# Four page products beside each other in the array, head pairs in alternation, and an input projection that starts before the norm

## The chip, the cores and the metric

The kernel runs on one core of one Trainium2 chip. The metric is the device time of one execution in microseconds, the median of several runs. TensorE (PE) multiplies, VectorE (DVE), ScalarE (ACT) and GpSimd (POOL) work element by element, SyncE (SP) issues most transfers.

## The reference

One inference step of a one-layer hybrid decoder, all in float32, for a prompt of 256 tokens and 8 samples of one new token each, whose 256 past keys and values lie in a paged cache (two pages of 128 rows per sample, 16 heads of 64):

```python
proj = rmsnorm(x, g_mix) @ w_in              # 1024 -> q, k, v, z, x/B/C, dt (IN_COLS)
q, k = rope(q), rope(k)
attn = softmax(q @ k.T / 8, causal) @ v      # prompt: own rows; sample: 2 pages of cache + its own new row
xbc  = silu(causal_conv(xbc)); dt = softplus(dt_raw + dt_bias)
y    = ssd_scan(xs, dt, -exp(a_log), B, C, state) + d_skip * xs
y    = group_rms(y * silu(z)) * g_ssd
x    = x + concat(rmsnorm(attn, g_attn), y) @ w_out
# PEER: 8 heads, two product keys of 128, top 16 of 16384 experts per token
x    = x + sum_e softmax_e * gelu(xn . u_e) * v_e
y_out = rmsnorm(x, g_final)                  # also out: new k, v, conv and ssd states
```

For the prompt all 16384 experts are computed densely and weighted; for the samples the chosen rows are gathered.

## The kernel before

Tokens lie along the free axis (264 columns: 256 of the prompt, 8 samples), features along the 128 partitions in 8 chunks. The order of each engine is written out by hand; semaphores tie the engines together.

- **Opening.** ScalarE squares the input `res`, TensorE sums the squares over partitions with a matrix of ones (L466, 8 products), VectorE makes `rstd`, scales the input into `xn` (L903), TensorE forms dt (L471). Then `tile(i)` (L481): 8 products of a 128x128 weight tile from `ring` (four slots, loaded by SyncE) with `xn` into bank `pj[i % 2]`; ScalarE copies it to `proj` (`copy`). Twelve tiles are the convolution's channels (VectorE's `conv`), with small turns and products after tiles 4 and 6. SyncE writes the decay rows and the B/C rows to memory and reads them back spread over all partitions (`wide`), between its tile loads.
- **Chunk loop.** For each of 8 chunks `c` (two heads): four tiles (q, k, v, z), between them `expand`, `turn_probs`, `ends`, `attend` of the chunk before, and at the end `mixed` (the scan's three products for each head) and `scores` (L494 to L496). Each head's results use half of the array's rows or columns.
- **Page stage.** After the loop 32 cache pages of 512 KB pass through six slots (`pages`, `NS = 6`): SyncE's `page(n)` waits until page `n - 6` is used, loads the physical page number from `ptab`, and issues the transfer. `key_pages` (L602) gives the scores of one sample's 16 heads against its two pages (16 rows of output, 256 columns); VectorE and ScalarE make its softmax (`sample_max`, `sample_probs`); `value_pages` (L635) multiplies by the values, with the probabilities padded into 128 columns of which one sample's 16 are not zero, so that all samples add up in two banks. Among them stand the sums of the two norms (L654, L657). VectorE's chain from these sums to the split operands (`mix_low`, L1188) precedes the output projection.
- **Output projection.** `out_half` (L671), 16 weight tiles, each split in a high and a low part by ScalarE and GpSimd. `values` (L681) after its first half tile picks each sample's heads out of `v6`.
- **PEER.** Query tiles and keys, then `up` (L1521) and `down` (L1551) over all experts. Before group `GX` of `down` stands `samples` (L1571, L1582): the samples' residual and their gathered rows, 8 rows of output.

## Time and profile before

| | us |
|---|---|
| median of 3 runs (lowest, highest) | 1233.85 (1231.4, 1236.24) |
| the profiled execution's own time | 1229.45 |
| its span | 1227.3 |
| TensorE busy | 1199.8 |
| VectorE, ScalarE, GpSimd busy | 785.8, 571.5, 753.8 |

The profiled execution lies 4.4 us below the median of the runs. Busy time of TensorE says that it had an instruction in flight, not that its array was full. In the profile every float32 product stands as two instructions, so that `x16` are eight products. PEclk 1.00 is 2.4 GHz, 0.50 is 1.2 GHz.

### The profile page before, as it was taken

The page shows a single profiled execution, that of the slowest core. Times are in us where ns is not written, and L with a number is a line of the kernel's source. Part 1 is how long each engine was busy: PE and PEld are TensorE (multiplying, and loading weights), DVE is VectorE, ACT ScalarE, POOL GpSimd, SP SyncE. Part 2 cuts the span into 40 slices and gives each one's busy share as a digit, 9 for nine tenths or more (in the row PEclk, how much of TensorE's full clock was granted, in tenths as well). Part 3 has the DMA queues.
Part 4 walks back from the last instruction along what each step waited for, and adds up shares of the span by engine and source line. Part 5 has one row for each costly group of instructions (what it writes and reads, how often), then busy time and mean ns, then how long its engine had stood idle before and what let it go on. Part 6 is the DMA issues. An engine that isn't in the chain of part 4 may idle for free.

```text
span 1227.3 us, 23601 instructions
## 1 busy us (share of the span) xinstructions
PE 1199.8 (98%) x7463; PEld 1039.8 (85%) x7463; DVE 785.8 (64%) x1749; ACT 571.5 (47%) x1287; POOL 753.8 (61%) x622
## 2 busy tenths in 40 slices
PE   7999999999999999999999999999999999999997
PEld 5877888745988899999999999998888888888766
DVE  4579787666139999400599999994544555666334
ACT  3222323252435555556555554444555555555435
POOL 0058241003835599998776767666776798798645
PEclk9999999999999999999999999999999999999999
DMA  6565575287645276666544444444665697788523
GB/s 210 164 214 148 166 257 155 88 288 272 184 150 156 88 224 190 188 186 182 162 141 144 142 142 140 145 140 145 189 189 188 188 325 259 238 282 269 184 97 111
DMA packets 99863, 224.88 MB, mean 183 GB/s; under 512 B 11682, under 2 KB 12306, under 8 KB 99274
## 3 DMA queue, kind: packets, MB, share of 16 engines
q1 hardware_dynamic: 96762, 214.52, 56.2%
q0 software_dynamic: 2304, 8.39, 2.0%
q10 hardware_dynamic: 720, 1.01, 0.2%
q8 instruction: 40, 0.66, 0.2%
q14 instruction: 37, 0.30, 0.1%
HBM read 215.61 MB, written 8.19 MB: 182 GB/s over the span
## 4 chain that ended last, share of the span: by engine, by line
PE 68%; issue 1%; POOL 1%; DVE 0%; ACT 0%; DVEq 0%; POOLq 0%; ACTq 0%
PE bank L1551 29%; PE bank L1521 28%; PE bank L1531 5%; PE bank L1474 2%; PE bank L1486 1%; PE bank L1582 1%; PE bank L1498 1%; POOL hl L1399 1%; PE bank L1571 0%; POOL hl L1414 0%; DVE acts L1941 0%; ACT acts L1751 0%; PE bank L1600 0%; PE bank L1564 0%; DVEq L1319 0%
## 5 line engine op out<-in xcount | busy, mean ns | idle before, releaser
L1399 POOL TENSOR_TENSOR hl<-ring,hl 128x512 fp32r<-128x512 f32 x448 | 586.1, 1319 | 195.1 <-ACT hl L1631 186.2
L1631 ACT CAST hl<-ring 128x512 fp32r<-128x512 f32 x512 | 316.8, 620 | 301.0 <-PE bank L1551 168.0
L1521 PE MATMUL bank<-split,hl 128*128 128x256 f32 x3072 | 378.7, 282 | 0.5 <-ACT hl L1631 0.3
L1521 PEld LDWEIGHTS bank<-split,hl 128*128 128x128 f32 x3072 | 366.3, 188 | 1.2 <-POOL hl L1399 0.6
L1551 PE MATMUL bank<-hl,split 128*128 128x512 f32 x1524 | 353.6, 394 | 0.0
L1551 PEld LDWEIGHTS bank<-hl,split 128*128 128x128 f32 x1524 | 285.9, 188 | 67.8 <-issue 0.9
L481 PE MATMUL pj<-xn,ring 128*128 128x264 f32 x704 | 165.0, 390 | 1.4 <-DMA ring<-in_w_ring 1.4
L1911 DVE TENSOR_TENSOR split<-acts,split 128x256 fp32r<-128x256 f32 x128 | 128.1, 1022 | 50.3 <-ACT split L1727 46.5
L481 PEld LDWEIGHTS pj<-xn,ring 128*128 128x128 f32 x704 | 132.3, 192 | 25.7 <-issue 2.8
L1918 DVE TENSOR_TENSOR hl<-ring,hl 128x512 fp32r<-128x512 f32 x64 | 45.1, 705 | 119.8 <-ACT hl L1631 119.8
L457 POOL TENSOR_TENSOR wo<-ring,wo 128x512 fp32r<-128x512 f32 x32 | 46.9, 1473 | 95.5 <-ACT wo L856 95.4
L433 POOL TENSOR_TENSOR hs<-hs,dds 128x256 f32<-128x256 f32 x32 | 22.7, 739 | 116.9 <-DVE xdt L1091 75.5
L1877 DVE TENSOR_SCALAR bv<-bkey,ig 128x130 f32<-128x130 f32 x256 | 86.0, 394 | 0.0
L1886 DVE TENSOR_TENSOR acts<-acts,bank 128x244 f32<-128x244 f32 (+31 forms) x64 | 66.3, 1036 | 19.5 <-PE bank L1531 19.2
L1698 ACT ACTIVATE acts<-bank 128x256 f32<-128x256 f32 (+31 forms) x124 | 41.1, 332 | 67.3 <-PE bank L1521 67.2
L1531 PE MATMUL bank<-bv,av 128*128 128x128 f32 x512 | 67.4, 274 | 0.0
L1531 PEld LDWEIGHTS bank<-bv,av 128*128 128x128 f32 x512 | 62.4, 191 | 0.0
L1414 POOL TENSOR_TENSOR hl<-ring,hl 128x512 fp32r<-128x512 f32 x24 | 31.0, 1301 | 35.9 <-ACT hl L1641 35.7
L1727 ACT CAST split<-acts 128x256 fp32r<-128x256 f32 x128 | 51.0, 401 | 0.2 <-DVE acts L1894 0.2
L728 ACT COPY proj<-pj 128x264 f32<-128x264 f32 x44 | 16.6, 376 | 68.7 <-PE pj L481 68.7
L1894 DVE TENSOR_TENSOR acts<-acts,gtmp 128x256 f32<-128x256 f32 (+32 forms) x67 | 42.0, 626 | 8.4 <-ACT gtmp L1700 8.4
L1873 DVE TENSOR_TENSOR av<-bank,ig 128x512 f32<-128x512 f32 x64 | 43.3, 677 | 0.0
(339 smaller groups left out, 1218.4 us busy)
## 6 DMA issues: line engine op xcount, KB each, us to landing
ring<-in_uv SPq DMA_DIRECT2D x256, 256.0 KB, 2.7
ring<-in_v_rows SPq DMA_DIRECT2D x256, 256.0 KB, 3.1
ring<-in_w_ring SPq DMA_DIRECT2D x76, 512.0 KB, 3.7
room<-in_cache_k SPq DMA_DIRECT2D x16, 512.0 KB, 5.3
room<-in_cache_v SPq DMA_DIRECT2D x16, 512.0 KB, 4.7
hs<-in_state_ssm SPq DMA_DIRECT2D x8, 512.0 KB, 4.7
out_ssm_s<-hs SPq DMA_DIRECT2D x8, 512.0 KB, 5.8
acts<-x_rows SPq DMA_DIRECT2D x8, 512.0 KB, 5.5
```

The source lines that it names most:

```text
L457: nc.gpsimd.tensor_tensor(wo[:, n % HL, 1], raw_o[:, n % RAW], wo[:, n % HL, 0].bitcast(F32), ALU.subtract).then_inc(o_lo, 1)
L481: mm = nc.tensor.matmul(pj[i % 2][:, 0:NT], ring[:, s, k], xn[:, k], start=(k == 0), stop=(k == KD - 1))
L1399: nc.gpsimd.tensor_tensor(hl[:, r % HL, 1], raw[:, r], hl[:, r % HL, 0].bitcast(F32), ALU.subtract).then_inc(lo_done, 1)
L1521: mm = nc.tensor.matmul(out, hl[:, r % HL, m, k * P:(k + 1) * P], split[:, x, kk, 0:TP], start=(kk == 0 and n == 0), stop=(kk == KD - 1 an ...
L1531: mm = nc.tensor.matmul(rb[m % 2][:, j * P:(j + 1) * P], av[:, m % 2, j], bv[:, m % 2, j, 0:P], start=True, stop=True)
L1551: mm = nc.tensor.matmul(acc[2 * k + half][:], split[:, p, 2 * s + a, k * P:(k + 1) * P], hl[:, r % HL, m], start=False, stop=False)
L1631: nc.scalar.copy(hl[:, r % HL, 0], raw[:, r]).then_inc(hi_done, 1)
L1727: nc.scalar.copy(split[:, g % 2, 2 * n, 0:TP], acts[:, g * GRP + n, :]).then_inc(wg_hi, 1)
L1877: hot = nc.vector.tensor_scalar(bv[:, m % 2, j], bkey[:, :, 0:BW // BR], ig[:, 0, at:at + 1], ig[:, 2, at:at + 1], ALU.is_equal, ALU.mult)
L1886: nc.vector.tensor_tensor(a, a, rb[m % 2][:].rearrange("p (t c) -> p t c", t=TG)[:, :, 0:R0 + m + 1], ALU.mult).then_inc(g_out, 1)
L1911: nc.vector.tensor_tensor(split[:, p, 2 * s + 1, 0:TP], acts[:, g * GRP + s, :], split[:, p, 2 * s, 0:TP].bitcast(F32), ALU.subtract).then ...
L1918: nc.vector.tensor_tensor(hl[:, r % HL, 1], raw[:, r], hl[:, r % HL, 0].bitcast(F32), ALU.subtract).then_inc(lo_dve, 1)
```

## The change

Six things are changed.

1. The first two tiles (and dt) use `xg`, the input times `g_mix` alone; VectorE multiplies their results by `rstd` (`evict_early`), in place of ScalarE's copy. The squares are added on VectorE, so that one product sums them. Eighteen 128x128 products of `pick` with itself stand first on TensorE.
2. The small products after tile 4 stand after tile 6, those after tile 6 after tile 7. ScalarE, not SyncE, issues the three row transfers.
3. In `scores`, `attend` and `mixed` the two heads alternate from product to product; `attend` and `mixed` now write 64 rows of output for each head in place of 128.
4. Pages are worked in fours: a batch is page `g` of four samples, and the four products go to output partitions 0, 32, 64 and 96, 16 rows each. The batch's pages are released together (`mm.then_inc(page_used, SIDE)`). A sample's own new key joins the softmax at the end, by two factors per sample and head (`sample_rates`, `sample_factors`) which `spread_rates` spreads over the partitions.
5. The values of the first four samples are picked by `values(0)` before the output projection, the others and the factors after its first half tile.
6. In `samples` the eight samples go to four output positions, two rows each; the banks are cleared first.

```diff
+SIDE, SPAN = 4, 32
+NQ = NB // SIDE
...
-                    b, g = n // NPG % NB, n % NPG
+                    q, g, j = n // (NPG * SIDE) % NQ, n // SIDE % NPG, n % SIDE
+                    b = q * SIDE + j
...
-                    if i == 10:
-                        sp.wait_ge(bc_copied, 1)
-                        sp.dma_start(t["bc_rows"].rearrange("a b n -> b a n"), brow).then_inc(bc_kept, 16)
...
-                        sp.wait_ge(bc_kept, 16)
-                    if i == 9:
-                        sp.wait_ge(acs_ready, 1)
-                        sp.dma_start(t["acs_rows"], acs[:]).then_inc(acs_kept, 16)
...
+                for j in range(SIDE):
+                    sp.dma_start(sel6[j * SPAN:j * SPAN + NH], t["sel"]).then_inc(sel6_in, 16)
...
+                        if i == 0:
+                            pe.wait_ge(xg_done, k + 1)
+                        if i == 2 and k % 4 == 0:
+                            pe.wait_ge(normed, k // 4 + 1)
+                        mm = nc.tensor.matmul(pj[i % 2][:, 0:NT], ring[:, s, k], (xg if i < 2 else xn)[:, k], start=(k == 0), stop=(k == KD - 1))
                     mm.then_inc(ring_used[s], 1)
+
+                pe.wait_ge(picked, 2)
+                flat = pick[:].rearrange("p c h -> p (c h)")
+                for n in range(18):
+                    nc.tensor.matmul(yb[:, 0:P], flat, flat, start=True, stop=True)
+                tile(0)
+                pe.wait_ge(cst_in, 16)
+                pe.wait_ge(pre1, 1)
+                nc.tensor.matmul(hd[0][:, 0:NT], ones, sq[:, 0], start=True, stop=True).then_inc(summed, 1)
+                pe.wait_ge(wdt_in, 16)
+                for k in range(KD):
+                    mm = nc.tensor.matmul(hd[1][0:NH, 0:NT], wdt[:, k], xg[:, k], start=(k == 0), stop=(k == KD - 1))
+                mm.then_inc(dt_ready, 1)
...
+                    for q0, q1, k1, at in ((0, P, P, 0), (P, TP, TP, P)):
+                        for j in range(2):
+                            r = slice(j * HD, (j + 1) * HD)
+                            mm = nc.tensor.matmul(hd[j][:, at:at + k1], proj[r, Q0 + c, q0:q1], proj[r, K0 + c, 0:k1], start=True, stop=True)
+                            if q0:
+                                mm.then_inc(s_ready, 1)
...
-                                         ).then_inc(o_ready, 1)
+                    for n, (k, at) in enumerate(((0, 0), (0, P), (1, P))):
+                        for j in range(2):
+                            r = slice(j * HD, (j + 1) * HD)
+                            if n == 0:
+                                pe.wait_ge(pt_copied, 2 * c + j + 1)
+                            mm = nc.tensor.matmul(hd[j][r, at:at + P], vtok[:, k, r], pt[:, j, n * P:(n + 1) * P],
+                                                  start=(n < 2), stop=(n != 1))
+                            if n == 2:
...
+                    for n, k in enumerate((0, 1, 1)):
+                        for j in range(2):
+                            r, at = slice(j * HD, (j + 1) * HD), j * TP + k * P
+                            mm = nc.tensor.matmul(yb[r, at:at + P], h0[:, r] if n == 2 else xtok[:, k, r],
+                                                  cs[:, j] if n == 2 else wgt[:, j, k * P:(k + 1) * P], start=(n < 2), stop=(n != 1))
...
-                    if i == 4:
+                    if i == 6:
...
+                def key_batch(n):
+
+                    q, g = n // NPG, n % NPG
+                    batch_in(n)
+                    for c in range(KD):
+                        for j in range(SIDE):
+                            mm = nc.tensor.matmul((swb, yb)[q][j * SPAN:j * SPAN + NH, g * P:(g + 1) * P],
+                                                  q6[:, q * SIDE + j, c * NH:(c + 1) * NH],
+                                                  pages[:, (n * SIDE + j) % NS, c * P:(c + 1) * P], start=(c == 0), stop=(c == KD - 1))
+                    mm.then_inc(page_used, SIDE)
...
+                def value_batch(n):
+
+                    q, g = n // NPG, n % NPG
+                    pe.wait_ge(pts_ready, q + 1)
+                    batch_in(NQ * NPG + n)
+                    for m in range(2):
+                        for j in range(SIDE):
+                            mm = nc.tensor.matmul(o6_bank[q][m][j * SPAN:j * SPAN + NH], pt6[:, q, g, j * SPAN:j * SPAN + NH],
+                                                  pages[:, ((NQ * NPG + n) * SIDE + j) % NS, m * 4 * P:(m + 1) * 4 * P],
+                                                  start=(g == 0), stop=(g == NPG - 1))
...
+                key_batch(0)
+                turn_probs(KD - 1)
+                key_batch(1)
+                attend(KD - 1)
                 pe.wait_ge(y_done, KD)
...
+                key_batch(2)
                 pe.wait_ge(o_copied, 2 * KD)
...
+                turn_sample_probs(0)
+                key_batch(3)
+                value_batch(0)
+                value_batch(1)
+                turn_sample_probs(1)
...
+                value_batch(2)
+                value_batch(3)
...
+                def values(q):
+
+                    pe.wait_ge(v6_masked, 2 * q + 2)
...
+                values(0)
                 for d in range(6):
...
-                        values()
+                        values(1)
+                        spread_rates()
...
+                    if i == 8:
+                        act.wait_ge(acs_ready, 1)
+                        act.dma_start(t["acs_rows"], acs[:]).then_inc(acs_kept, 16)
+                        act.wait_ge(bc_ready, 1)
+                        nc.scalar.copy(brow.rearrange("b a n -> b (a n)"), hd[0][0:NB]).then_inc(bc_copied, 1)
+                        act.wait_ge(bc_copied, 1)
+                        act.dma_start(t["bc_rows"].rearrange("a b n -> b a n"), brow).then_inc(bc_kept, 16)
+                    if i == 10:
+                        act.wait_ge(bc_kept, 16)
+                        act.wait_ge(dd_done, 1)
+                        act.dma_start(wide, t["bc_rows"].rearrange("(o a) b n -> o (a b n)", o=1).broadcast_to([P, 2 * GROUPS * NB * P])
+                                      ).then_inc(bc_in, 16)
...
+                for n in range(4):
+                    dve.wait_ge(x_in[n], 16)
+                    for k in (2 * n, 2 * n + 1):
+                        nc.vector.tensor_scalar(xg[:, k], res[:, k], par[:, P_GMIX + k:P_GMIX + k + 1], None, ALU.mult).then_inc(xg_done, 1)
+                    if n:
+                        dve.wait_ge(squared, n + 1)
+                        link(nc.vector.tensor_tensor(sq[:, 0:2], sq[:, 0:2], sq[:, 2 * n:2 * n + 2], ALU.add))
+                nc.vector.tensor_tensor(sq[:, 0], sq[:, 0], sq[:, 1], ALU.add).then_inc(pre1, 1)
                 dve.wait_ge(summed, 1)
...
+                def evict_early(i):
+
+                    dve.wait_ge(ring_used[i], 2)
+                    nc.vector.tensor_tensor(proj[:, CT[i]], pj[i][:, 0:NT], rstd[:, 0], ALU.mult).then_inc(early_out, 1)
...
+                def sample_rates():
+
+                    dve.wait_ge(exp6, NQ)
+                    dve.wait_ge(own_copied, 1)
+                    link(nc.vector.tensor_tensor(s6[:, 6], s6[:, 0], s6[:, 3], ALU.max))
+                    nc.vector.tensor_tensor(s6[:, 4], s6[:, 0], s6[:, 6], ALU.subtract).then_inc(diffs6, 1)
...
+                def sample_factors():
+
+                    dve.wait_ge(rates6, 1)
+                    link(nc.vector.tensor_tensor(s6[:, 7], s6[:, 2], s6[:, 4], ALU.mult))
+                    link(nc.vector.tensor_tensor(s6[:, 7], s6[:, 7], s6[:, 5], ALU.add))
...
+                def values_kept(q):
+
+                    dve.wait_ge(page_used, N_PAGES - (NQ - 1 - q) * SIDE * NPG)
+                    dve.wait_ge(hs_out[1 + q], 16 * (KD // HS))
...
+                                                ALU.mult).then_inc(v6_masked, 1)
...
+                values_kept(0)
...
+                        pe.wait_ge(smp_zero, 2)
+                        for k in range(KD):
+                            for j in range(SIDE):
+                                nc.tensor.matmul(smp[k // 4][j * SPAN:j * SPAN + NQ, k % 4 * P:(k % 4 + 1) * P], res[:, k, TP + j:NT:SIDE], ident,
+                                                 start=(k % 4 == 0), stop=False)
+                        pe.wait_ge(wz_done, 2)
+                        for q in range(NQ):
                             for half in range(2):
...
+                                    b = q * SIDE + j
+                                    if half == 0:
+                                        pe.wait_ge(rows_in[b], 32)
+                                    mm = nc.tensor.matmul(smp[half][j * SPAN:j * SPAN + NQ], wz[:, b],
+                                                          rows8[:, b, half * (D // 2):(half + 1) * (D // 2)], start=False, stop=(q == NQ - 1))
...
```

TensorE's order in a round of the chunk loop. Before (`att` in the L511 rows is `vtok` and `pt`, `ssd` is `xtok` and `wgt`):

```order
L511 MATMUL hd<-att 128x128
L512 MATMUL hd<-att 128x128
L513 MATMUL hd<-att 128x128
L511 MATMUL hd<-att 128x128
L512 MATMUL hd<-att 128x128
L513 MATMUL hd<-att 128x128
L481 MATMUL pj<-xn,ring 128x264 x8
L545 MATMUL yb<-ssd 128x128
L546 MATMUL yb<-ssd 128x128
L547 MATMUL yb<-ssd,h 128x128
```

And now, with the scores behind it:

```order
L513 MATMUL hd<-att 64x128 x6
L465 MATMUL pj<-xn,ring 128x264 x8
L548 MATMUL yb<-ssd 64x128 x4
L548 MATMUL yb<-ssd,h 64x128 x2
L490 MATMUL hd<-cst,proj 128x128 x2
L494 MATMUL hd<-proj 128x128 x2
L494 MATMUL hd<-proj 128x256 x2
```

The number of products is the same; neighbours now belong to different heads and write 64 partitions each.

TensorE from the end of the pages to the output projection. Before (`xn` and `bcb` hold the squares, `hs` the padded probabilities and then `v6`, `room` the pages):

```order
L654 MATMUL swb<-xn,cst 128x264
L654 MATMUL yb<-xn,cst 128x264
L657 MATMUL hd<-bcb,cst 128x256
L635 MATMUL bcp<-room,hs 128x512
L635 MATMUL xbp<-room,hs 128x512
```

Nine more such pairs of L635 follow before, and then the projection (L671) at once. Now:

```order
L616 MATMUL hd<-cst,hs 128x128 x2
L656 MATMUL pj<-xn,cst 128x264 x2
L659 MATMUL hd<-bcb,cst 128x256
L626 MATMUL swb<-room,hs 16x512 x4
L626 MATMUL yb<-room,hs 16x512 x4
L626 MATMUL swb<-room,hs 16x512 x4
L626 MATMUL yb<-room,hs 16x512 x4
L682 MATMUL hd<-cmx,hs 128x4 x8
L672 MATMUL pj<-mixr,wo 128x264 x24
L682 MATMUL hd<-cmx,hs 128x4 x8
L691 MATMUL hd<-fe,bcb 128x16 x8
```

Two batches are left behind the sums, and `values(0)` (L682) has moved ahead of the projection's first half tile.

VectorE between the norm sums and the value masks, now:

```order
L1209 TENSOR_SCALAR att<-pj 128x264 x2
L1211 RECIPROCAL att<-att 128x528
L1213 TENSOR_SCALAR att<-hd 128x256
L1214 RECIPROCAL att<-att 128x256
L1217 SCALAR_TENSOR_TENSOR mix<-mix,par,att 128x264 x8
L1221 SCALAR_TENSOR_TENSOR mix<-mix,par,att 128x256 x8
L1186 TENSOR_TENSOR s<-s 128x2
L1187 TENSOR_TENSOR s<-s 128x2
L1188 RECIPROCAL s<-s 128x2
L1189 TENSOR_TENSOR s<-s 128x2 x2
L1192 TENSOR_SCALAR fe<-cmx,s 128x4 x4
L1228 TENSOR_TENSOR mixr<-mix,mixr 128x1056 x2
```

The nine small instructions from L1186 to L1192 are new there; behind the last row stand the two masks of `values_kept(0)`, for which `values(0)` waits.

## Rows read from the trace of the kernel before

**Rows 1.** The page's line of TensorE: busy time, share, instructions.
```profile
PE 1199.8 (98%) x7463; PEld 1039.8 (85%) x7463; DVE 785.8 (64%) x1749; ACT 571.5 (47%) x1287; POOL 753.8 (61%) x622
```
**Rows 2.** Windows: stretch, its length, busy us by engine, PEclk, DMA share, GB/s.
```profile
69.83:239.22 169.39, 164.31 (x862) 137.20 (x862) 135.50 (x363) 47.30 (x159) 70.54 (x98) 1.00 0.54 168
239.22:301.67 62.45, 62.45 (x266) 30.62 (x265) 41.26 (x111) 25.82 (x52) 5.69 (x1) 1.00 0.78 263
```
**Rows 3.** Timeline of TensorE and VectorE, opening: start, us, instruction, [idle before, releaser].
```profile
5.35 5.67 PE L466 MATMUL hd<-bcb,cst 128*128 128x264 f32 x16 [5.35 <-ACT bcb L720]
11.13 0.43 DVE L899 TENSOR_SCALAR rstd<-hd 128x264 f32<-128x264 f32 x1 [9.85 <-PE hd L466]
11.60 1.80 DVE L900 RECIPROCAL rstd<-rstd 128x264 f32<-128x264 f32 x1
...
18.18 2.05 PE L481 MATMUL pj<-xn,ring 128*128 128x264 f32 x8
```
**Rows 4.** Windows round the clock's two falls, columns as in rows 2.
```profile
36.30:39.84 3.54, 2.26 (x23) 2.24 (x23) 3.37 (x13) 1.27 (x3) 0.00 (x0) 1.00 0.78 294
39.90:43.20 3.30, 3.30 (x9) 2.58 (x9) 2.81 (x10) 0.05 (x1) 0.00 (x0) 0.50 0.04 15
...
353.90:357.30 3.40, 3.40 (x8) 2.68 (x9) 3.13 (x17) 2.53 (x8) 0.00 (x0) 0.50 0.84 299
```
**Rows 5.** Timeline of TensorE at the first tile of the chunk loop.
```profile
69.83 3.83 PE L481 MATMUL pj<-xn,ring 128*128 128x264 f32 x16 [1.35 <-DMA ring<-in_w_ring]
```
**Rows 6.** Timeline of TensorE and VectorE, one round of the chunk loop.
```profile
215.22 0.38 PE L545 MATMUL yb<-ssd 128*128 128x128 f32 x2
...
216.56 0.27 PE L494 MATMUL hd<-cst,proj 128*128 128x128 f32 x1
216.76 0.48 PE L495 MATMUL hd<-proj 64*128 64x128 f32 x2
...
218.72 3.83 PE L481 MATMUL pj<-xn,ring 128*128 128x264 f32 x16
...
224.83 0.35 DVE L1080 TENSOR_SCALAR att<-att,astat 128x256 f32<-128x256 f32 x1
...
226.16 0.82 PE L504 MATMUL hd<-cst,att 128*128 128x128 f32 x6
```
**Rows 7.** Timeline of TensorE at the first sample's key pages.
```profile
239.22 0.56 PE L609 MATMUL bcp<-qk,pick 128*16 128x8 f32 x16
239.64 3.61 PE L602 MATMUL swb<-room,up 128*16 128x256 f32 x16
```
**Rows 8.** Group of one bank's value products, by form, busy us and mean ns.
```profile
L635 PE MATMUL bcp<-room,hs 128*128 128x512 f32 x32 | 16.6, 599 | 0.0
```
**Rows 9.** SyncE's timeline, two page loads after a release.
```profile
243.98 0.35 SPq L350 DMA_DIRECT2D room<-in_cache_k  x1
...
245.09 0.35 SPq L350 DMA_DIRECT2D room<-in_cache_k  x1
```
**Rows 10.** Tile room, 243.9 to 246.5: the two loads from issue to landing, us.
```profile
DMA to landing us min/median/max: 3.6/4.0/4.4
```
**Rows 11.** Timeline of VectorE and TensorE, from norm sums to output projection.
```profile
284.67 0.43 DVE L1167 TENSOR_SCALAR att<-swb 128x264 f32<-128x264 f32 x1 [4.17 <-PE yb L654]
...
297.36 3.55 DVE L1188 TENSOR_TENSOR mixr<-mix,mixr 128x1056 fp32r<-128x1056 f32 x3
...
301.67 3.81 PE L671 MATMUL pj<-mixr,wo 128*128 128x264 f32 x24
302.27 0.69 DVE L1198 TENSOR_TENSOR hs<-bcp,cmx 128x512 f32<-128x512 f32 x1 [0.23 <-PE xbp L635]
...
305.31 1.85 PE L681 MATMUL hd<-cmx,hs 128*128 128x8 f32 x16
```
**Rows 12.** Timeline of TensorE at the samples' expert products.
```profile
1160.43 1.91 PE L1571 MATMUL bank<-cst,res 128*8 128x128 f32 x16
1162.18 13.90 PE L1582 MATMUL bank<-acts,wz 128*8 128x512 f32 x32
```

More of the change, by code:

```diff
@@ L591, in _, with batch_in @@
                     scores(c)
-                def key_pages(first, end):
-                    for b in range(first, end):
-                        n = b * NPG
-                        if b >= 2:
-                            pe.wait_ge(exp6, b - 1)
-                        for g in range(NPG):
-                            pe.wait_ge(page_full[(n + g) % NS], 16 * ((n + g) // NS) + 16)
-                        for c in range(KD):
-                            mm = nc.tensor.matmul((swb, yb)[b % 2][0:NH, 0:PAST], q6[:, b, c * NH:(c + 1) * NH],
-                                                  pages[:, n % NS:n % NS + NPG, c * P:(c + 1) * P], start=(c == 0), stop=(c == KD - 1))
-                        mm.then_inc(page_used, NPG)
+                def batch_in(n):
+                    for j in range(SIDE):
+                        page = n * SIDE + j
+                        pe.wait_ge(page_full[page % NS], 16 * (page // NS) + 16)
@@ L606, in _ @@
                 pe.wait_ge(q_spread, 3)
                 pe.wait_ge(picked, 2)
+                pe.wait_ge(pj_copied, N_IN - 1)
                 for c in range(KD):
-                    mm = nc.tensor.matmul(bcp[0:NH, 0:NB], pick[:, c], qk6[:, c], start=(c == 0), stop=(c == KD - 1))
+                    for j in range(SIDE):
+                        mm = nc.tensor.matmul(pj[0][j * SPAN:j * SPAN + NH, 0:NQ], pick[:, c], qk6[:, c, j::SIDE],
+                                              start=(c == 0), stop=(c == KD - 1))
@@ L628, in value_pages @@
-                def value_pages(first, end):
-                    for b in range(first, end):
-                        for g in range(NPG):
-                            n = (NB + b) * NPG + g
-                            pe.wait_ge(page_full[n % NS], 16 * (n // NS) + 16)
-                            for m, bank in enumerate((bcp, xbp)):
-                                mm = nc.tensor.matmul(bank[:], pad6[:, g, b], pages[:, n % NS, m * 4 * P:(m + 1) * 4 * P],
-                                                      start=(b == 0 and g == 0), stop=(b == NB - 1 and g == NPG - 1))
-                            mm.then_inc(page_used, 1)
@@ L652, in _ @@
+                pe.wait_ge(own_copied, 1)
+                pe.wait_ge(pj_copied, N_IN)
                 pe.wait_ge(pre_s, 1)
-                for n, bank in enumerate((swb, yb)):
-                    mm = nc.tensor.matmul(bank[:, 0:NT], ones, sq_ssd[:, 4 * n], start=True, stop=True)
+                for n in range(GROUPS):
+                    mm = nc.tensor.matmul(pj[n][:, 0:NT], ones, sq_ssd[:, 4 * n], start=True, stop=True)
                 mm.then_inc(sum_s, 1)
@@ L837, in _ @@
                 nc.scalar.activation(sq_att[:, :, 0:TP], mix[:, 0:KD, 0:TP], ACT.Square).then_inc(sq_p, 1)
-                for b in range(4, 7):
-                    sample_exps(b)
+                sample_exps(1)
                 act.wait_ge(gated, 1)
@@ L981, in _ @@
                                           ).then_inc(cb_copied, 1)
-                for i in range(7, CONV_CH):
+                for i in range(8, CONV_CH):
                     conv(i)
@@ L1959, in _ @@
                         if g == GX + 1:
-                            norm(TT, NB, 2)
+                            norm(TT, P, 2)
                         if g == GX + 2:
-                            scale(TT, NB, 1, smp)
+                            scale(TT, P, 1, smp)
+                        if g == GD + NB:
+                            dve.wait_ge(gelu_done, NKEY)
+                            for bank_s in smp:
+                                nc.vector.memset(bank_s[:], 0.0).then_inc(smp_zero, 1)
                         if g == GD + NB + 1:
```

291 lines of the change are left out of this document (119 added, 172 removed).

## The prediction

> **What bounds the kernel now.** I read the page's busy times first: TensorE is busy 98% of the span [rows 1], the others 64% at most. So time goes only where TensorE's work shrinks or where it starts to wait. Second, the windows by stage: in the chunk loop it is busy 164.3 of 169.4 us, in the page stage 62.45 of 62.45, while the transfer engines are 78% busy there [rows 2]. Third, the timeline at each changed place [rows 3, 5 to 9, 11, 12], for what one group takes and how far its inputs are ahead of it, and the windows round the places where the clock falls [rows 4]. The change touches the first 307 us and one place near 1160; everything else should keep its time.
>
> **Opening.** TensorE starts its norm sums at 5.35, is done at 11.0, and then stands behind VectorE (0.43 + 1.80 us, the root, the scaling) until tile 0 at 18.18 [rows 3]. Now tile 0 wants only the scaled input: eight scalings of 264 columns at the 0.43 of L899, with three additions of twice that width between them, about 4.5 us from the first arrival near 5, so tile 0 runs from about 9.5 to 13. The squares' product and dt's eight follow (a tile's pace, 0.46 us a product [rows 5]: 4.1), so tile 1 starts near 17.1 where it started at 18.18 + 3.66 = 21.8: 4.7 us won. The root is ready by then, so dt, not the norm, is what VectorE is late for. Three losses may go besides: 1.28 us idle among the small products after tile 4 (2.26 busy of 3.54), the half clock behind it (3.3 us at 0.50, so 1.7 lost) [rows 4], and 1.35 us for a weight tile that SyncE had issued late, behind its waits for rows [rows 5]. That is 4.3. Against it: tile 5 waits for ScalarE's copy of tile 3, which stands behind the dt chain; with two more multiplications and the scaling to `xn` in that chain I count 1.1 us of new wait. Sum -7.9; I take -7. The eighteen products end before the input is scaled, if they run at 0.22 us each in full clock or 0.44 at half, and cost nothing; what they buy is that tile 0 is not at half clock. If it is, 1.7 go back: bounds -3 and -9. The three row transfers moved to ScalarE stand ahead of `copy(8)` and `copy(10)`; ScalarE is busy 47 of 169 us later on [rows 2] and has two banks of slack, so I put nothing on them.
>
> **Chunk loop, eight rounds.** `mixed` takes 216.56 - 215.22 = 1.34 us for six products, `attend` the same, `scores` 218.72 - 216.56 = 2.16 [rows 6]. If two heads' products run side by side, the first two fall to 0.67 each, and the scores to two turns (0.44), 128 and 256 columns (0.66) and 0.15 for changing rows, 1.25. Eight times 0.67, seven times 0.67 and eight times 0.9 are 17.3. No row shows two products side by side. The lower end is 17.3 won; at the other end nothing is won and each alternation costs what the step from whole to half array costs now: L495 comes 0.20 after the turn and a 128-column product takes 0.32 to 0.22 elsewhere, 0.1 each, 16 a round, 13 us lost. I take -15, near the full overlap, since the products name disjoint rows or columns. The other engines must keep up with a round of 18.2 us in place of 20.5: VectorE's last probabilities are ready at 225.2, TensorE takes them at 226.16 [rows 6]. Both score banks now come at the end, which costs VectorE 0.5 of that 1.0; the rest holds.
>
> The Trainium skill, page TensorEngine Tiling (Array Packing), Key Properties, says that changing the tiling mode drains TensorE. The trace agrees with the 0.1 us above. By it a batch, whose four products share one mode, pays once and not at each product, and the sum stands.
>
> **Page stage.** Let S be the end of the last scores (239.22 before). Before, a sample's keys take 3.45 us (16 instructions of 256 columns, 0.216 each), and its two pages are released while the next sample's are there; TensorE never waits [rows 2, 7]. Now a batch of keys is 64 instructions of 128 columns, 6.9 us in a row, 1.7 with four side by side; the small product of L609 shows 26 ns an instruction (16 in 0.42 us), so issue allows 1.7 too. A batch of values is 16 instructions of 512 columns, the form of [rows 8], at twice 0.216 again 6.9 or 1.7. But four pages are held until a batch ends, there are six slots, and the next batch needs two pages that are not yet asked for. What that costs stands in the trace: the release at 239.64 + 3.45 = 243.1, the first load issued 243.98, the second 1.11 later [rows 9], landing 4.4 after its issue [rows 10], is 6.4 us from release to start. It is hidden before and open now. A cycle is 6.4 + 1.8 = 8.2 us, seven of them follow the first batch, whose pages were fetched in the loop. With the own-key products (64 instructions, 1.7) the pages end at S + 1.7 + 1.8 + 7 x 8.2 = S + 60.9, before S + 62.45. So nearly all of 41 us of spared array time turns into waits for pages.
>
> Then the clock: it fell after 1.28 us of idling in 3.5 [rows 4], and here TensorE idles 6.4 of 8.2. At half clock a batch takes 3.4, the cycle 9.8, the end is S + 72.1.
>
> The sums of the norms stand after the sixth batch: S + 44.5, at half clock S + 52.5, plus a turn and three products, S + 46.3 or S + 56.0. From their readout VectorE needs 284.67 to 299.7 (two of L1188's three at 1.18 each), 15.1 us [rows 11], and now also 3 small instructions for the rates, 9 for the factors (0.15 to 0.2 each, 2.1 together) and the two masks at 0.65: 18.6. `values(0)` can start at S + 65.0 or S + 74.6, later than the pages end either way: the wait for pages is replaced by VectorE's chain as what the projection starts on. `values(0)` 1.85, the half tile 3.64, `values(1)` and the spreading 1.85 each [rows 11] give S + 74.2, or S + 86.6 with the first groups at half clock. Before, the same point is at 307.0, S + 67.8. The stage costs +6.4 or +18.8; with idle stretches this long I take +15, nearer the half clock. Bounds: +3, if loads land at the fastest 3.6, and +43, if nothing overlaps.
>
> **Samples in PEER.** 1160.43 to 1176.1 is 15.6 us [rows 12]. Now 64 instructions of 128 columns and 32 of 512: 6.9 + 13.8 in a row, a quarter of it 5.2, with some loss 6.6. -9; +5 if nothing overlaps. The clearings and the four-fold stores lie beside TensorE, which nothing waits for.
>
> The Trainium skill, page TensorE: Matmul & The Clock Gate, Part 3, gives a measured gain of 3.07 for four row tiles and 2.38 for three column tiles. No run here shows either. By 3.07 a batch is 2.25 us and not 1.7, and the time would come out about 4 us later.
>
> **Sum.** -7 - 15 + 15 - 9 = -16 on the profiled execution's 1229.45, which gives 1213.5. That execution lies 4.4 under the median of the runs, so on their scale 1233.85 - 16, about 1218.
>
> **Rivals.**
> - *The clock stays up in the page stage.* For it: the falls seen are few, and turns and head products stand in the gaps. Against it: the 1.28 us idle of rows 4 sufficed. Then the stage costs +6.4: 1233.85 - 24.6, about 1209. Faster landings point the same way.
> - *Head pairs don't overlap, fours do, and the opening gives half.* The products of two heads wait for each other by rows or by a shared bank (`mixed` writes one bank). -4 + 0 + 15 - 9 = +2: about 1236.
> - *Nothing overlaps: slower.* Column positions then only cut the work into more instructions, and the place is the page stage: a cycle is 6.4 + 6.9 = 13.3, the pages end at S + 8.6 + 93.1 = S + 101.7, the projection is past its groups at S + 110.9, +43. With -7 in the opening, 0 in the loop and +5 in the samples +41: about 1275. The point from which this decides: the page stage eats the other gains (31 us) once a batch takes more than 5.4 us (7.1 for the first with the own-key products ahead, 7 x 11.8 behind it, 9.2 of projection: S + 98.9). For it: no row of before has two products in flight on different parts of the array. Against it: the positions are disjoint in rows or columns, and so are the outputs.
>
> **How the numbers follow.** The forecast 0.47, clock up 0.25, pairs alone failing 0.15, nothing overlapping 0.13. A measurement can tell 0.5%, 6 us. Faster by more: nearly all of the first two and a fifth of the third, 0.74. Within: 0.08. Slower: the fourth and a third of the third, 0.18. The range goes from 1203 (clock up, loop at its full 17, samples at 5.2) to 1243 (pairs failing, page stage worse by some us); left out are the fourth and little else. The likeliest case's own range is 1207 to 1231.
>
> **What would show it.** In the opening: tile 0 before 10, tile 12 near 62. In the loop a round of 18.2 us, the six products of `mixed` in 0.7. In the page stage gaps of about 6 us before each batch, ended by transfers of the cache pages, PEclk under 1.00 from the second batch on, batches of 1.7 to 3.5; before `values(0)` an idle time ended by VectorE's mask. At the samples some 6 us. It is wrong if the batches follow each other without waiting for pages, if a batch takes 7 us, or if pairs of heads take 1.3 us as before.

## Result and the profile of the changed kernel

The changed kernel takes 1225.74 us, median of four runs (1224.55 to 1227.1); the kernel before took 1233.92 beside it. The ratio is 0.9947 (95% interval 0.9928 to 0.9966): 6.5 us faster by the ratio, 8.2 by the medians, where 16 were forecast. The direction and the places were right; the size was half of the forecast by the medians, and less by the ratio.

The profiled execution took 1227.1 us, with a span of 1225.2. The page's line of busy times, to be held against [rows 1]:

```profile
PE 1156.1 (94%) x7713; PEld 1019.4 (83%) x7713; DVE 793.4 (65%) x1725; ACT 565.3 (46%) x1266; POOL 744.0 (61%) x621
```

TensorE's work shrank by 43.7 us and the span by 2.1: nearly all of what was spared turned into waiting. Windows of the loop and of the page stage, columns as in [rows 2], say where:

```profile
60.54:219.82 159.28, 152.17 (x863) 122.26 (x861) 133.56 (x364) 47.38 (x161) 66.41 (x97) 1.00 0.56 182
219.82:299.93 80.11, 34.23 (x431) 18.93 (x429) 39.56 (x72) 21.31 (x33) 6.26 (x4) 0.71 0.67 231
```

The loop is 10.1 us shorter. The page stage is 17.7 us longer, though TensorE works 34.2 us in it and not 62.5: it stands idle for the other 46, and its granted clock over the stage is 0.71. The timeline of TensorE there answers to [rows 7, 8, 11]:

```profile
219.82 0.67 PE L636 MATMUL pj<-qk,pick 128*16 128x2 f32 x64
220.50 1.94 PE L607 MATMUL swb<-room,up 128*16 128x128 f32 x64
...
228.81 3.62 PE L607 MATMUL swb<-room,up 128*16 128x128 f32 x64 [3.85 <-DMA room<-in_cache_k]
...
240.52 3.46 PE L607 MATMUL yb<-room,up 128*16 128x128 f32 x64 [6.78 <-DMA room<-in_cache_k]
...
250.47 3.60 PE L607 MATMUL yb<-room,up 128*16 128x128 f32 x64 [6.12 <-DMA room<-in_cache_k]
260.99 1.91 PE L626 MATMUL bcp<-room,hs 128*16 128x512 f32 x8 [6.92 <-DMA room<-in_cache_v]
...
274.74 1.06 PE L656 MATMUL pj<-xn,cst 128*128 128x264 f32 x4
...
292.19 1.91 PE L626 MATMUL swb<-room,hs 128*16 128x512 f32 x8 [7.41 <-DMA room<-in_cache_v]
...
297.37 2.70 PE L682 MATMUL hd<-cmx,hs 128*128 128x4 f32 x16 [1.96 <-DVE hs L1240]
299.93 5.49 PE L672 MATMUL pj<-mixr,wo 128*128 128x264 f32 x24
```

Read the first batch and the second. Both are 64 instructions; the first takes 1.94 us, where a row of them would take 6.9 by the prediction's estimate, so the four do run side by side. The second takes 3.62: the same work with a granted clock of 0.50 (window 228.81 to 232.40). Ahead of it TensorE waits 3.85 us for pages, ahead of each later batch 4.9 to 7.4, and at the end 1.96 us for VectorE.

The opening, against [rows 3], and the samples, against [rows 12]:

```profile
1.40 5.86 PE L471 MATMUL yb<-pick 128*128 128x128 f32 x36 [1.40 <-DVE pick L916]
8.53 3.83 PE L465 MATMUL pj<-mix,ring 128*128 128x264 f32 x16 [1.27 <-DMA ring<-in_w_ring]
...
1168.58 1.93 PE L1635 MATMUL bank<-cst,res 128*2 128x128 f32 x64
1170.33 3.62 PE L1644 MATMUL bank<-acts,wz 128*2 128x512 f32 x32
1173.88 0.96 PE L1607 MATMUL bank<-hl,split 128*128 128x512 f32 x3
```

Tile 0 begins 9.65 us earlier, and the samples take 5.3 us and not 15.6. The projection's first full group starts at 308.95, 89.1 us behind the last scores, where it was 67.8.

One more reading, since it would mislead. The span is only 2.1 us shorter because this execution lost 4.0 us in the last loop: from its first product (853.04) to the samples it took 315.54 us, where the kernel before took 311.55 and `warm` (below), with the same code there, 311.54. Two rows, a timeline and a window, show where:

```profile
1021.80 146.86 PE L1607 MATMUL bank<-hl,split 128*128 128x512 f32 x626 [2.17 <-DVE hl L1980]
1021.80:1025.60 3.80, 3.80 (x10) 2.98 (x11) 0.69 (x1) 0.62 (x1) 0.16 (x1) 0.55 0.71 201
```

TensorE waited 2.17 us for VectorE, and the granted clock was 0.55 in the 3.8 us behind that, which is where the other 1.8 us went. Of the twelve other profiles only that of `open_only` has it too, 2.77 us at the same product, so it is a loss of some executions and not of the change. The median of the runs is what counts.

### The profile page after: what moved, and what is told of

Same layout as the page of the kernel before. It is cut to its first block, busy times and chain, and to the rows that moved or that the text cites. A ratio compares the mean times of both kernels' runs of the same rounds, so it can differ in the third digit from the quotient of the medians.

```text
span 1225.2 us, 24078 instructions
## 1 busy us (share of the span) xinstructions
PE 1156.1 (94%) x7713; PEld 1019.4 (83%) x7713; DVE 793.4 (65%) x1725; ACT 565.3 (46%) x1266; POOL 744.0 (61%) x621
## 4 chain that ended last, share of the span: by engine, by line
PE 68%; issue 1%; DVE 1%; POOL 0%; ACT 0%; DVEq 0%; POOLq 0%; ACTq 0%
PE bank L1577 30%; PE bank L1607 29%; PE bank L1587 5%; PE bank L1530 2%; PE bank L1542 1%; PE bank L1554 1%; DVE split L1973 0%; PE bank L1627 0%; PE bank L1644 0%; POOL hl L1470 0%; DVE acts L2003 0%; PE bank L1635 0%; ACT acts L1813 0%; POOL hl L1455 0%; PE bank L1662 0%
## 5 line engine op out<-in xcount | busy, mean ns | idle before, releaser
L1973 DVE TENSOR_TENSOR split<-acts,split 128x256 fp32r<-128x256 f32 x128 | 134.8, 1079 | 39.1 <-ACT split L1789 35.4
L465 PE MATMUL pj<-xn,ring 128*128 128x264 f32 x672 | 156.8, 388 | 0.4 <-ACT proj L739 0.4
L465 PEld LDWEIGHTS pj<-xn,ring 128*128 128x128 f32 x672 | 125.0, 190 | 24.1 <-issue 4.3
L447 POOL TENSOR_TENSOR wo<-ring,wo 128x512 fp32r<-128x512 f32 x32 | 42.2, 1326 | 134.1 <-ACT wo L877 134.1
L427 POOL TENSOR_TENSOR hs<-hs,dds 128x256 f32<-128x256 f32 x32 | 21.3, 695 | 106.2 <-DVE xdt L1134 66.2
L1530 PE MATMUL bank<-split,hl 128*128 128x264 f32 x288 | 37.3, 287 | 0.0
```

What stands on the lines that cost most here:

```text
L465: mm = nc.tensor.matmul(pj[i % 2][:, 0:NT], ring[:, s, k], (xg if i < 2 else xn)[:, k], start=(k == 0), stop=(k == KD - 1))
L1530: mm = nc.tensor.matmul(qb[s][:, 0:NT], hl[:, n % HL, m, k * P:(k + 1) * P], split[:, x, 4 * a + k], start=(a + kind + k == 0), stop=(a + ...
L1973: nc.vector.tensor_tensor(split[:, p, 2 * s + 1, 0:TP], acts[:, g * GRP + s, :], split[:, p, 2 * s, 0:TP].bitcast(F32), ALU.subtract).then ...
```

## Experiments

A ratio is against runs of the kernel before on the same chip; us are medians. A difference from the changed kernel is one between medians taken at different times, and the kernel before moved from 1233.9 to 1231.6 over these times, so such a difference of 3 us or less says little. "S" is the start of the own-key products (the end of the last scores).

### The page stage as before, the rest as changed

```diff
-key_batch(0); turn_probs(KD - 1); key_batch(1); ...   # four samples side by side
+key_pages(0, 1); key_pages(1, 2); turn_probs(KD - 1); ...   # one sample after another, as before
```

> Opening, loop and samples as changed; the page stage as before. Theory A (the page stage costs 21 us against the one of before, and its neighbours don't depend on it): projection d = 1 begins 67.8 us behind the last scores in place of 89.1, time 1225.7 - 21.3 = 1204, within 1201 to 1208. Theory B (the pages arrive no faster whatever TensorE does, and the stage grew by about 10 us only because the loop ahead of it became 10 us shorter): the stage stays near 80 us, time 1215 to 1220. Theory C (what is won ahead is given back in the later loops): 1210 or more with a page stage of 68.

Measured: 1203.35 us, ratio 0.9755 (0.9737 to 0.9773). Window of the stage:

```profile
224.35:288.06 63.71, 63.58 (x266) 30.36 (x265) 41.73 (x112) 25.71 (x52) 5.70 (x1) 0.97 0.77 264
```

The stage is back to 63.7 us with no waits, and its first full group comes at S + 69.0. So this part of the change costs 1225.74 - 1203.35 = 22.4 us (23.7 by the ratios), and the other three parts gain 29.7 (forecast: 31). Theories B and C fall: nothing was given back elsewhere.

### What the batches wait for: slots or bytes

```diff
-sp.dma_start(pages[:, n % NS], cache[bass.ds(at, 1)]...)
+sp.dma_start(pages[:, n % NS, 0:D // 2], cache[bass.ds(at, 1), :, 0:D // 2]...)
```

> Only the first 512 columns of each page are loaded (256 KB in place of 512), and the products read these twice: half the bytes, all else the same. Theory A (latency from release to landing): the landing falls from 3.6 to 5.4 us to 3 to 4, the gaps from 6.5 to about 5, the cycle from 10.2 to about 8.8. Theory B (bytes over the transfer engines): the cycle halves, 5 us.

Measured: 1216.91 us (one run; the kernel leaves out the second half of each page and reads the first twice), and windows of 240 to 270, first of the changed kernel, then of this one:

```profile
240.00:270.00 30.00, 10.89 (x146) 6.49 (x146) 5.22 (x8) 2.42 (x3) 0.00 (x0) 0.67 0.66 214
```
```profile
240.00:270.00 30.00, 14.37 (x118) 6.25 (x110) 7.26 (x15) 3.90 (x5) 0.00 (x0) 0.65 0.42 128
```

Batches start at 237.01, 245.75, 254.22, 262.99, 271.85 and 280.82: a cycle of 8.8 us against 10.3, as theory A said, with the transfer engines busy 0.42. Half the bytes took away 15% of the cycle. What is waited for is the way from a release through SyncE's issue to the landing, and not the transfer engines' throughput.

The counterpart keeps the bytes and frees the slots earlier:

```diff
-pages = part(room, 0, NS, D)                 # 6 slots, 4 held to the end of a batch
+pages = part(room, 0, 2 * NS, D // 2)        # 12 half slots
+for half in range(2): half_in(m); ...; mm.then_inc(page_used, SIDE)
```

> Each page comes in two transfers of 256 KB into twelve half slots, and TensorE gives four half slots back in the middle of a batch; the products are the same. Theory A (the batch waits from the release of its slots to the landing, 6.4 us, because four of six slots are held to its end): eight half slots are then under way while four are read, the gaps of 6 to 7 us fall under 3, the cycle from 10.2 us to the 6 to 7 that four pages of 512 KB take, the pages end 25 us earlier, VectorE's chain becomes the end of the stage, and 10 to 15 us of it show: 1211 to 1216. Theory B (the transfer engines bound the stage): the cycle stays near 10 us and the time within 3 us of 1225.7.

Measured: 1213.15 us, 0.9846 (0.9824 to 0.9868), 12.6 us better than the changed kernel. A window of its page stage, and two rows of TensorE at its end:

```profile
240.00:260.00 20.00, 9.76 (x92) 3.37 (x96) 4.80 (x7) 2.42 (x3) 0.00 (x0) 0.50 0.92 306
```
```profile
274.60 1.91 PE L633 MATMUL yb<-room,hs 128*16 128x512 f32 x8 [3.88 <-DMA room<-in_cache_v]
285.64 3.55 PE L689 MATMUL hd<-cmx,hs 128*128 128x4 f32 x16 [9.13 <-DVE hs L1247]
```

With the slots free, the transfer engines are 0.92 busy, yet nine half batches still wait 1.7 to 3.9 us for pages. Whether bytes or SyncE's issue bound them now was not separated: in this trace SyncE needs 1.1 us for a transfer whose page number it loads and 0.52 for one whose number is there, so 6.5 us for the eight of a batch (an estimate), against a cycle of 7.5 us. The pages end at S + 56.8 in place of S + 75.6, 18.8 us earlier, and only 12.6 reach the end, for TensorE then waits 9.13 us for VectorE.

### What half clock costs there

Ahead of each batch but the first stand 30 products (20 and 24 at two places):

```diff
+for x in range(30): nc.tensor.matmul(bank[:, 3 * P:4 * P], flat, flat, start=True, stop=True)
 key_batch(2)
```

> Some 30 small products into a free bank ahead of each batch's wait for pages (about 4.9 us of TensorE work at full clock, where it idles 6 to 7 us). Theory A (half clock is part of the cost): the granted clock stays 1.00 through the page stage, a batch takes 1.9 us and not 3.5, seven batches and the first groups of the projection give 5 to 9 us back: 1217 to 1221. Rival (the stage ends on landings and on VectorE's chain, the products' pace matters little): clock 1.00 but within 2 us of 1225.7. If the products run at half clock, they take 9.8 us and the time grows by 20.

Measured: 1218.75 us, 0.9886 (0.9868 to 0.9903): 7.0 us better than the changed kernel.

```profile
249.15 1.94 PE L607 MATMUL yb<-room,up 128*16 128x128 f32 x64
251.03 6.96 PE L615 MATMUL pj<-pick 128*128 128x128 f32 x60
257.92 1.05 PE L631 MATMUL bcp<-room,hs 128*16 128x512 f32 x8
258.79 1.04 PE L631 MATMUL xbp<-room,hs 128*16 128x512 f32 x8
```

A batch takes 1.94 us and the cycle 8.9. Thirty products took 6.96 us and not 4.9, since each is two instructions; they just filled the wait. They also give a row to hold a batch against: 60 instructions of 128 columns in 6.96 us, so 7.4 for 64.

The 7.0 us, a third of the stage's cost, are not all that half clock takes. The clock is 0.99 from 230 to 291 and the pages end at S + 65.7, 9.9 us earlier; then TensorE waits 5.11 us for VectorE, and behind that wait the clock is 0.60 again until 309, so that the first groups of the projection take as long as before. A half-speed batch also holds its slots 1.7 us longer.

### VectorE's chain

```diff
 sample_rates()
+sample_factors()
 ...
-sample_factors()
 for n in (2, 3): mix_low(...)
```

> The changed kernel with the nine small VectorE instructions of the factors put straight behind the three of the rates, ahead of the readout of the norm sums; nothing else moves. In the changed kernel they took 5.2 us (1.06 to 1.52 us each pair or four) while GpSimd ran its subtractions for the first weights, where the same form takes 0.15 elsewhere. Theory A (the two engines are in each other's way, and VectorE's chain ends the stage): at the new place the nine take 1 to 2 us, 3 to 4 us of the chain go, time 1221.5 to 1223. Rival 1 (they are slow of themselves, since each waits for the one before): still 5 us at the new place, time 1225.7. Rival 2 (the last pages end the stage and not VectorE): small ones fast, time within 1 us of 1225.7.

Measured: 1221.22 us (1216.56 to 1225.75), 0.9921 (0.9896 to 0.9945). That is 4.5 better than the changed kernel by the medians and 3.2 by the ratios, whose intervals overlap, so the gain in time is not clear of noise. VectorE at these instructions, first in the changed kernel, then here:

```profile
288.39 1.23 DVE L1186 TENSOR_TENSOR s<-s 128x2 f32<-128x2 f32 x1
289.65 1.19 DVE L1187 TENSOR_TENSOR s<-s 128x2 f32<-128x2 f32 x1
290.88 0.17 DVE L1188 RECIPROCAL s<-s 128x2 f32<-128x2 f32 x1
```
```profile
278.55 0.16 DVE L1186 TENSOR_TENSOR s<-s 128x2 f32<-128x2 f32 x1 [0.27 <-ACT s L864]
278.75 0.16 DVE L1187 TENSOR_TENSOR s<-s 128x2 f32<-128x2 f32 x1
278.94 0.17 DVE L1188 RECIPROCAL s<-s 128x2 f32<-128x2 f32 x1
```

The first half of theory A holds: the multiplication of two columns takes 1.2 us beside GpSimd's subtractions and 0.16 where GpSimd rests; the reciprocal, with one input, takes 0.17 at both places; all nine take 5.2 us there and 1.3 here. The Trainium skill, page SBUF — State Buffer, section "SBUF: two separate sides", has a rule for this: a VectorE instruction with two inputs from SBUF and a GpSimd instruction that reads SBUF lock their shared pair of ports for the whole instruction, and the other one is blocked. The trace agrees, the untouched reciprocal included.

The second half, that 3 to 4 us of this reach the end, is not shown. In the changed kernel TensorE waited only 1.96 us for VectorE; here it waits for none, since the last pages end at S + 76.7 and are now the limit, and `values(0)` begins 0.9 us earlier by S. What else this profile gains is the clock behind it:

```profile
298.22 1.95 PE L682 MATMUL hd<-cmx,hs 128*128 128x4 f32 x16
300.03 3.15 PE L672 MATMUL pj<-mixr,wo 128*128 128x264 f32 x24
```

These took 2.70 and 5.49 us in the changed kernel, at a granted clock of 0.50 in the second. The profiled execution is the fastest of six that spread over 9 us.

Both remedies together, with the norm sums one value batch earlier:

```diff
 value_batch(0)
-value_batch(1)
 turn_sample_probs(1); ...  # and the three products of the norm sums
+value_batch(1)
```

> The half slots of the run before, with two moves in order: the three products of the norm sums and the turn of the second group's probabilities one value batch earlier, and the factors as in factors_early. In halves TensorE waited 9.13 us for VectorE ahead of values(0) while the sums' inputs were ready at 255.2 and their products ran at 262.1. Theory A (after the slots VectorE's chain ends the stage): 6 us from the sums and 4 from the factors, the wait of 9 gone, then the pages are the end: projection begins 60 us behind the last scores in place of 69.4, time 1203 to 1207. Rival (the chain has another late start, ScalarE's casts or GpSimd's subtractions): less than 4 us, 1209 or more.

Measured: 1202.81 us, 0.9767 (0.9741 to 0.9793). The projection starts at S + 62 and VectorE is no longer waited for. Three things are changed at once here; their shares were not taken apart. The projection's first full group comes at S + 69.7, no earlier than with the old page stage (S + 69.0).

```profile
276.79 1.91 PE L633 MATMUL yb<-room,hs 128*16 128x512 f32 x8 [2.78 <-DMA room<-in_cache_v]
278.63 3.58 PE L689 MATMUL hd<-cmx,hs 128*128 128x4 f32 x16
282.06 4.43 PE L679 MATMUL pj<-mixr,wo 128*128 128x264 f32 x24
```

Two runs add small products to keep the clock up:

```diff
+if 2 * n + m >= 5: warm(8)      # early_light; early_warm: warm(16) ahead of all eight
 half_in(at)
```

> early_sums with 16 small products ahead of each of the eight half batches of values (1.9 us at full clock, where 2 to 4 us are waited). Theory A (half clock still costs at the end of the stage: values(0) 3.55 us in place of 1.85, the half tile 4.9 for 3.8, the spreading 2.8 for 1.85, the first group 5.4 for 3.15): full clock there gives 4 to 6 us: 1198 to 1202. Rival (the added products delay the pages' release, since the transfers are 0.92 busy): the same as early_sums or 2 to 4 us more.

> early_sums with eight small products ahead of each of the last three half batches of values only (16 instructions, 1.9 us each time at full clock as early_warm showed them, against waits of 0.8 to 3.3). Theory A (half clock in values(0) and the half tile costs 3 us): 1199.5 to 1201. Rival (they push back the last half batches, since the clock is at half there and they take 3.8 us): 1203 or more.

Sixteen ahead of each half batch gave 1215.62 us, 0.9883 (0.985 to 0.9915), 12.8 worse than without. They took 3.84 us each time, twice my figure (I had again counted a product as one instruction), so TensorE did not wait for pages any more but came late for them. Eight ahead of the last three gave 1201.86 us (1199.37 to 1202.39), 0.9753 (0.9729 to 0.9777): the best version of all, but not to be told from `early_sums` or from the old page stage (1203.35).

### The loop and the opening by themselves

The kernel before, with `scores`, `attend` and `mixed` alternating the heads and nothing else changed. Of `attend`:

```diff
-                    for j in range(2):
-                        pe.wait_ge(pt_copied, 2 * c + j + 1)
...
+                    for n, (k, at) in enumerate(((0, 0), (0, P), (1, P))):
+                        for j in range(2):
...
```

> The kernel before with only the three functions of the chunk loop changed (scores, attend, mixed by alternating heads). Theory A (what the profile of the changed kernel shows: 10.1 us less between tile 12 and the last scores): 1233 - 10 = 1223. Rival (the forecast's 15 us are there and something else of the change takes 5 back): 1218. Rival (part is given back in the page stage, whose pages arrive no earlier): 1226 to 1228.

Measured: 1222.51 us, 0.9928 (0.99 to 0.9955), 8.9 us by the ratio, with an interval of 5.5 to 12.3. That excludes the forecast's 15; it holds theory A's 10, but also the 5 to 7 of the last rival. Rows of the changed kernel, against [rows 6]:

```profile
91.79 1.25 PE L513 MATMUL hd<-att 128*64 128x128 f32 x12 [0.57 <-ACT att L776]
...
217.79 0.66 PE L548 MATMUL yb<-ssd 128*64 128x128 f32 x8
218.28 0.39 PE L548 MATMUL yb<-ssd,h 128*64 128x128 f32 x4
218.60 0.44 PE L490 MATMUL hd<-cst,proj 128*128 128x128 f32 x2
218.97 0.93 PE L494 MATMUL hd<-proj 64*128 64x128 f32 x8
219.82 0.67 PE L636 MATMUL pj<-qk,pick 128*16 128x2 f32 x64
```

From start to start `mixed` takes 0.81 us (forecast 0.67) and the scores 1.22 (1.25). `attend` takes 0.81 only in the last two rounds of the loop; in the other five it takes 1.18. In the new order its second product already needs the second head's copy (`pt_copied`), and in the round shown ScalarE makes these two copies at 91.26 to 92.12, beside `attend` at 91.79; that this is the cause fits the rows and was not tested by itself.

The kernel before, with the opening alone changed (points 1 and 2 of the change):

> The kernel before with only the opening changed: first two tiles from the unscaled input, eighteen small products, tables of decay two tiles later, row transfers issued by ScalarE. Theory A (what the profile of the changed kernel shows, tile 0 9.65 us earlier and tile 12 9.3): the whole gain stays to the end, 1233 - 9 = 1224, within 1222 to 1226. Rival (the forecast's 7 us; the starts of one profiled run each differ by some us): 1226. Rival (part goes at the page stage or later): 1228 or more.

Measured: ratio 0.9938 (0.9914 to 0.9962), so 7.6 us. Two of seven runs took 2426 us, double the others, for no reason found; the median of the other five is 1224.31. Tile 0 begins at 9.54 here. The interval (4.7 to 10.6 us) holds both 7 and 9. Its profile gains less up to the chunk loop than that of the changed kernel did: 2.7 us less, 1.0 from the first weight tile, which landed later, and 1.7 from one tile at half clock, which the changed kernel ran in 3.83 us:

```profile
41.88 5.51 PE L467 MATMUL pj<-xn,ring 128*128 128x264 f32 x16
```

The eighteen small products left out of the changed kernel:

```diff
-for n in range(18): nc.tensor.matmul(yb[:, 0:P], flat, flat, start=True, stop=True)
```

> The changed kernel without the eighteen small products; all else the same. Theory A (they buy full clock for tile 0): the granted clock is at half until some 4 us after tile 0 begins, tile 0 takes 5.5 us or more in place of 3.83, tile 12 comes 1.7 to 2 us later and so does the end: 1227 to 1228. Rival (tile 1 waits on VectorE or on its weights anyway): no change, 1225.7. Rival (the small products delayed tile 0): faster by up to 1 us.

Measured: 1228.24 us, 0.9966 (0.9947 to 0.9985), 2.5 slower by the medians, but the intervals overlap (the changed kernel's ratio was taken at another time). The trace is clearer:

```profile
8.50 5.20 PE L465 MATMUL pj<-mix,ring 128*128 128x264 f32 x16 [8.50 <-DVE mix L919]
```

Tile 0 takes 5.20 us and not 3.83; the small products buy 1.4 us. Its first six instructions take 0.42 us each, where 0.23 is the pace of the changed kernel's tile 0. The profile's clock column reads 1.00 there all the same, so here the durations tell it and not that column.

## Why the prediction was half right

- **Opening, forecast -7.** Measured 7.6 by the ratio; 9.3 in the changed kernel's profile at tile 12. Tile 1 began at 16.39 and not 17.1, and the new wait behind tile 3's copy was 0.42 and not 1.1. Tile 0 at full clock was right. Part of the 9.3 is luck: the tile behind the small products ran at full clock in that profile and at half clock in `open_only`.
- **Loop, forecast -15: failed in size.** Measured 8.9 by the ratio, 10.1 in the profile. The overlap was there, but the array work fell by 12.1 us (164.3 to 152.2) and not 17.3. Two steps failed. The first is "the first two fall to 0.67 each": `mixed` takes 0.81, and `attend` 0.81 in two rounds and 1.18 in five. The second is "The other engines must keep up with a round of 18.2 us": waits grew by 2.0 us. A round without waits went from 20.8 (194.41 to 215.22 in the kernel before; the prediction's 20.5 was low) to 18.8. These terms add up to some 6 us of the 7.2 between 17.3 and 10.1; the rest is not placed.
- **Page stage, forecast +15: the right mechanism, mis-sized, and the largest miss.** Measured 22.4, and +21.3 in the profile (S + 89.1 in place of S + 67.8). The cycle (9.8 forecast, 10.3 on average), the half clock and VectorE's chain at the end are all in the text. Two things failed.
  - The choice between the two clocks, 3.8 us. I had computed +18.8 for half clock and took +15, "nearer the half clock"; the clock fell at the second batch.
  - The start of `values(0)`, forecast S + 74.6 and measured S + 77.6. The readout of the sums began at S + 56.0, as forecast. VectorE's chain behind it took 21.3 us and not 18.6, because I had priced its small instructions at 0.15 to 0.2 us, 2.1 for all twelve, from rows where GpSimd was idle, and the nine of the factors alone took 5.2. The pages were late too: they ended at S + 75.6 and not S + 72.1. So the right price for the nine would have made the forecast better, but taking them away can give back no more than the 1.96 us of waiting.
- **Samples, forecast -9.** In the profile -10.3.
- **Rivals.** Nothing overlapping and pairs failing are refuted by the 1.94 us of the first batch and the 0.81 of `mixed`. The clock did not stay up; `warm` gave 7.0 us back by holding it up in most of the stage. Even so the cycle was 8.9 and not 8.2, and the first full group came at S + 83.2, where the rival with the clock up had S + 74.2. Part of these 9 us is half clock, which `warm` leaves at the end of the stage; so the rival is not tested in full.
- **The skill's figures for packing.** The Trainium skill, page TensorE: Matmul & The Clock Gate, Part 3, gives 3.07 for four row tiles and 2.38 for three column tiles. These are four column tiles, and the rows give more: 6.9 / 1.94 = 3.6 for keys (7.4 / 1.94 = 3.8 by the row of `warm`) and 13.90 / 3.62 = 3.8 for the samples.

In sum, the page stage came out 7.4 us worse and the loop 5 to 6 us; the opening and the samples came out 2 to 4 us better than forecast together and hid a part of it. That the total still lies in the stated range of 1203 to 1243 says little, as the range is wide.

Still open: of the 29.7 us that the three good parts give together, the single ones give 7.6 + 8.9 + 10.3 = 26.8. The rest is inside the intervals.

## What to carry to other kernels

Before shrinking an engine's work, ask what the next limit is and how far off: here the stage had 62.45 us of TensorE work over transfers that were 0.78 busy, so a fourfold speed-up of the array could win some 13 us at most (an estimate: 0.22 of 62.45), and only if the slots came free as fast as before. No version here won any of it clear of noise: the best, `early_light`, has a ratio of 0.9753 and the old page stage 0.9755. Products that share a release hold all their buffers to the end, so give back parts. A price read off a small instruction holds only beside the same neighbours: see who else runs at its new place.

## What the runs showed of the hardware

- Products with outputs on four different 32-row parts of a bank run nearly fully side by side: 3.6 to 3.8 times as fast as in a row, by the rows above. Small ones gain too: 64 instructions of two columns take 0.67 us, 10 ns each, where 16 of eight columns took 0.42, 26 ns each.
- TensorE's granted clock can fall while TensorE is not idle. In `early_light` it is busy without a gap from 276 to 290, at first mostly with products of 4 and 16 columns; the granted clock then falls to 0.50, and a group of 3.15 us takes 5.63. Windows of 2 us:

```profile
280.00:282.00 2.00, 2.00 (x20) 2.00 (x19) 0.00 (x0) 1.08 (x2) 2.00 (x3) 1.00 0.85 303
282.00:284.00 2.00, 2.00 (x20) 2.00 (x20) 0.00 (x0) 0.00 (x0) 1.80 (x2) 1.00 0.85 221
284.00:286.00 2.00, 2.00 (x11) 2.00 (x11) 0.72 (x4) 0.00 (x0) 0.00 (x0) 0.50 0.68 186
```

  `early_warm` shows it behind a far longer busy stretch:

```profile
264.20:299.00 34.80, 34.80 (x295) 28.98 (x296) 18.72 (x27) 8.42 (x12) 12.76 (x6) 1.00 0.63 218
299.00:302.00 3.00, 3.00 (x20) 3.00 (x19) 0.00 (x0) 0.00 (x0) 0.64 (x1) 0.63 0.44 131
```

  The tile at 41.88 of `open_only` is a third case, behind 9.5 us without a gap. What makes the clock fall there is not shown: in `factors_early` the same four groups as in `early_light` follow one another from 298.22, and the clock stays at 1.00. The prediction's reading of [rows 4], a fall because of 1.28 us of idling, is therefore not certain either.

- In `halves`, transfers of 256 KB issued from 245.0 to 247.1, 0.5 us apart, each landed 0.65 to 0.7 us after the one before; at that pace, an estimate, a page of 512 KB takes 1.3 us and 26 pages 35 us, well under the 57 us at which the pages ended.
